# Two groups of expert gates behind every second late unit, four buffers of one-hots, and norm sums 128 columns wide

## The reference

```python
def rmsnorm(x, g):
    y = x * rsqrt(mean(x * x, axis=-1) + EPS)
    return y * g

def peer(h, w_query, sub_keys1, sub_keys2, expert_down, expert_up):
    # 8 heads, for each the best 16 of 128 x 128 experts by product keys
    ...
    gates = softmax(top_s)
    act = gelu(einsum("td,thkd->thk", h, expert_down[idx]))
    return einsum("thk,thkd->td", gates * act, expert_up[idx])
```

## Time and profile before

| | us |
|---|---|
| median of 3 runs (1384.83 to 1387.41) | 1386.22 |
| profiled execution, its own time | 1383.88 |
| its span in the trace | 1382.1 |
| TensorE busy | 1356.7 (98% of the span) |
| VectorE busy | 1032.1 (75%) |
| ScalarE busy | 863.1 (62%) |
| GpSimd busy | 652.3 (47%) |
| late stage, first to last `spread` | 804.6 to 1016.5 |

### The profile page before, as it was taken

The page is one execution under the profiler, slowest core; times in us unless marked ns, Lnnn a source line. Parts: engine busy times, 40 slices in busy tenths (PEclk is TensorE's granted clock), DMA queues, the critical chain, the costliest instruction groups (busy, mean ns, idle before and its releaser), DMA issues.

```text
span 1382.1 us, 30164 instructions
## 1 busy us (share of the span) xinstructions
PE 1356.7 (98%) x9200; PEld 1232.4 (89%) x9200; DVE 1032.1 (75%) x2272; ACT 863.1 (62%) x1825; POOL 652.3 (47%) x503
## 2 busy tenths in 40 slices
PE   7999999999999999999999999999999999999998
PEld 5799999999999988888888899999988888888886
DVE  7778868888888496548899678888876666666665
ACT  5668765555446666536666787777765555555554
POOL 4896793000005867698998887777720000000000
PEclk9999999999999999999999999999999999999998
DMA  9776565988883643565555554444456656666652
GB/s 340 279 253 225 203 241 183 332 323 320 334 331 119 215 138 107 183 229 182 183 196 184 182 169 153 154 160 157 152 167 196 189 193 196 191 191 195 194 188 89
DMA packets 79798, 283.83 MB, mean 205 GB/s; under 512 B 8821, under 2 KB 8949, under 8 KB 79610
## 3 DMA queue, kind: packets, MB, share of 16 engines
q1 hardware_dynamic: 79738, 283.07, 59.8%
HBM read 281.99 MB, written 1.05 MB: 205 GB/s over the span
## 4 chain that ended last, share of the span: by engine, by line
PE 66%; POOL 17%; issue 10%; DVE 4%; ACT 2%; DMA 1%; POOLq 0%; PEld 0%; PEldq 0%; SPq 0%; DVEq 0%
POOL w_lo L564 16%; PE psA L1868 15%; PE psA L1872 15%; PE psA L1871 15%; PE psD L1868 5%; PE psD L1871 5%; PE psD L1872 5%; PE psD L2363 1%; PE psD L2364 1%; PE psD L1918 1%; DVE arena L1549 1%; DMA xT<-x 1%; ACT w_hi L629 1%; DVE arena L1154 0%; PE psD L1921 0%
## 5 line engine op out<-in xcount | busy, mean ns | idle before, releaser
L629 ACT CAST w_hi<-raw 128x512 fp32r<-128x512 f32 x864 | 531.2, 620 | 430.6 <-PE psA L1868 251.3
L564 POOL TENSOR_TENSOR w_lo<-raw,w_hi 128x512 fp32r<-128x512 f32 x476 | 631.5, 1346 | 348.0 <-ACT w_hi L629 337.1
L1105 DVE TENSOR_TENSOR w_lo<-raw,w_hi 128x512 fp32r<-128x512 f32 x388 | 266.1, 691 | 152.6 <-ACT w_hi L629 151.3
L1868 PE MATMUL psA<-h_both,w_hi 128*128 128x256 f32 x960 | 279.5, 291 | 0.6 <-POOL w_lo L564 0.5
L1871 PE MATMUL psA<-h_both,w_hi 128*128 128x256 f32 x960 | 271.0, 282 | 0.0
L1872 PE MATMUL psA<-h_both,w_lo 128*128 128x256 f32 x960 | 270.9, 282 | 0.0
L1918 PE MATMUL psA<-h_both,w_hi 128*128 128x512 f32 x608 | 213.4, 396 | 0.4 <-POOL w_lo L564 0.4
L1868 PE MATMUL psA<-w_hi,u_hi 128*128 128x512 f32 x512 | 199.4, 389 | 0.4 <-DVE u_lo L1168 0.4
L1872 PE MATMUL psA<-w_hi,u_lo 128*128 128x512 f32 x512 | 199.2, 389 | 0.0
L1871 PE MATMUL psA<-w_lo,u_hi 128*128 128x512 f32 x512 | 199.2, 389 | 0.0
L1868 PEld LDWEIGHTS psA<-h_both,w_hi 128*128 128x128 f32 x960 | 183.4, 191 | 4.1 <-issue 1.5
(11 more groups left out here) (413 smaller groups left out, 2563.4 us busy)
## 6 DMA issues: line engine op xcount, KB each, us to landing
raw<-expert_down SPq DMA_DIRECT2D x128, 512.0 KB, 3.2
raw<-expert_up SPq DMA_DIRECT2D x128, 512.0 KB, 4.3
arena<-ada SPq DMA_DIRECT2D x96, 512.0 KB, 5.4
raw<-gateup SPq DMA_DIRECT2D x44, 512.0 KB, 5.4
raw<-feat SPq DMA_DIRECT2D x28, 512.0 KB, 3.7
raw<-win SPq DMA_DIRECT2D x24, 512.0 KB, 3.3
raw<-down SPq DMA_DIRECT2D x22, 512.0 KB, 6.0
raw<-wout SPq DMA_DIRECT2D x20, 512.0 KB, 3.3
```

Of the source, the lines that this page charges most:

```text
L564: nc.gpsimd.tensor_tensor(w_lo[:, s * HALF:(s + 1) * HALF], raw_half(n), w_hi[:, s * HALF:(s + 1) * HALF].bitcast(F32), ALU.subtract).then ...
L629: nc.scalar.copy(w_hi[:, n % SLOTS * HALF:(n % SLOTS + 1) * HALF], raw_half(n)).then_inc(hi_ready, 1)
L1105: V.tensor_tensor(w_lo[:, w], raw[:, n % 8 * HALF:(n % 8 + 1) * HALF], w_hi[:, w].bitcast(F32), ALU.subtract).then_inc(lo_ready, 1)
L1868: first = mm(o, w[0], m[0], start=start, stop=False, skip_group_check=True)
```

## The change

It makes four edits.

1. `GROUPS` goes from 2 to 4: four buffers of one-hots. Those of groups 0 to 3 are made ahead of the stage; VectorE's `group(g)` makes those of group g+4, and ScalarE lowers those of group k+4 behind the GELU of unit k (two groups each behind the last two units ahead of the stage).
2. TensorE makes no `spread` behind the first half of the even late units, and two behind that of the odd ones. The last two groups stay where they were.
3. The sums of `ssq_both` and of the final norm are 128 columns wide and not 2.
4. `keep_clock` with 2 matmuls ahead of `ssq_both`, and with 3 between the final sums and the final row spreads.

```diff
-        GROUPS = 2
-        hot = part(at_place("hot", M_AT, 2048, F16), 0, GROUPS, 2, GROUP, NK)
-        hot_lo = part(nc.alloc_sbuf_tensor_at("hot_lo", [P, 1024], F16, offset=late_at + 4 * 1024), 0,
+        GROUPS = 4
+        hot = part(at_place("hot", M_AT, 4096, F16), 0, GROUPS, 2, GROUP, NK)
+        hot_lo = part(nc.alloc_sbuf_tensor_at("hot_lo", [P, 2048], F16, offset=late_at + 4 * 1024), 0,
                       GROUPS, GROUP, NK)
...
                 if j >= P - LATE - 2:
-                    lower_hots((j - (P - LATE - 2)) * GROUP)
+                    for g in range(2):
+                        lower_hots(((j - (P - LATE - 2)) * 2 + g) * GROUP)
...
                 for j in range(4):
                     activate_late()
-                    lower_hots(i * (4 * GROUP) + (j + 2) * GROUP)
+                    lower_hots(i * (4 * GROUP) + (j + GROUPS) * GROUP)
...
             for j in range(3):
                 activate_late()
-                if j < 2:
-                    lower_hots(T - (2 - j) * GROUP)
...
-            one_hots(0)
-            one_hots(GROUP)
+            for g in range(GROUPS):
+                one_hots(g * GROUP)
...
                 gate_experts(g * GROUP)
-                one_hots(g * GROUP + 2 * GROUP)
+                one_hots(g * GROUP + GROUPS * GROUP)
                 multiply_late(late)
...
-            gate_experts(T - 2 * GROUP)
-            gate_experts(T - GROUP)
+            for g in range(N_GROUPS - GROUPS, N_GROUPS):
+                gate_experts(g * GROUP)
+                if g < N_GROUPS - 2:
+                    multiply_late(P - LATE + g)
...
                     for t in range(NT):
-                        last = mm(b[:, 2 * t:2 * t + 2], src[:, j, t * P:(t + 1) * P], weights[:, j, :],
+                        last = mm(b[:, t * P:(t + 1) * P].rearrange("p (n c) -> p n c", c=2),
+                                  src[:, j, t * P:(t + 1) * P],
+                                  weights[:, j, :].unsqueeze(1).broadcast_to([P, P // 2, 2]),
...
             first_banks = [Dr.bank(), Dr.bank()]
+            keep_clock(first_banks[0], 2)
             ssq_both(xn2, both_w, lambda: keep_clock(first_banks[0], 5))
...
-            for _ in range(LATE % LATE_TURN - 2):
-                unit(A, h_parts, beside=spread)
+            def spread_two(h):
+                if h == 0:
+                    spread(0)
+                    spread(0)
+            for k in range(LATE % LATE_TURN - 2):
+                unit(A, h_parts, beside=spread_two if k % 2 else None)
             with repeat(pe, LATE // LATE_TURN, {halves: 2 * LATE_TURN, A.count: LATE_TURN, groups: LATE_TURN}):
-                for _ in range(LATE_TURN):
-                    unit(A, h_parts, beside=spread)
+                for k in range(LATE_TURN):
+                    unit(A, h_parts, beside=spread_two if k % 2 else None)
...
-                    done = mm(psA[:, 0, 2 * t:2 * t + 2], U[:, j, t * P:(t + 1) * P], ones[:, 0:2],
+                    done = mm(psA[:, 0, t * P:(t + 1) * P], U[:, j, t * P:(t + 1) * P], ones[:, :],
...
             done.then_inc(sem("final_sums"), 1)
+            keep_clock(psA[:, BANKS - 1, :], 3)
             pe.wait_ge(sem("final_inverse"), 1)
```

More of the change, by code:

```diff
@@ L655, in roots_of @@
                     b = psA[:, A_AT[name] % BANKS, :]
-                    sums = b[:, 0:2 * NT].rearrange("p (t c) -> p c t", c=2)
+                    sums = b[:, 0:T].rearrange("p (t c) -> p c t", c=P)
                     nc.scalar.activation(roots[:, 0, :], sums[:, 0, :], ACT.Sqrt,
@@ L1064, in _ @@
             act.wait_ge(sem("final_sums"), 1)
-            nc.scalar.activation(roots[:, 0, :], psA[:, 0, 0:2 * NT].rearrange("p (t c) -> p c t", c=2)[:, 0, :],
+            nc.scalar.activation(roots[:, 0, :], psA[:, 0, 0:T].rearrange("p (t c) -> p c t", c=P)[:, 0, :],
                                  ACT.Sqrt, bias=eps[:, 0:1]).then_inc(sem("final_roots"), 1)
@@ L1785, in _ @@
             TURN = 12
-            at = N_GROUPS - 2 - (N_GROUPS - 2) // TURN * TURN
+            at = (N_GROUPS - GROUPS) % TURN
             for g in range(at):
                 group(g, P - LATE + g)
-            with repeat(dve, (N_GROUPS - 2 - at) // TURN, {hots: TURN, gates_n: TURN, late_n: TURN}) as i:
+            with repeat(dve, (N_GROUPS - GROUPS) // TURN, {hots: TURN, gates_n: TURN, late_n: TURN}) as i:
                 for g in range(TURN):
                     group(i * TURN + (g + at), i * TURN + (P - LATE + at + g))
-            gate_experts(T - 2 * GROUP)
-            gate_experts(T - GROUP)
+            for g in range(N_GROUPS - GROUPS, N_GROUPS):
+                gate_experts(g * GROUP)
+                if g < N_GROUPS - 2:
+                    multiply_late(P - LATE + g)
             lows.n = 2 * (UNITS - DVE_LOWERS)
```

## The result

The changed kernel takes 1400.85 us (median of 4 runs, 1399.8 to 1402.59), the kernel before 1386.82 (median of 4). The ratio is 1.0102, 95% interval 1.0085 to 1.0119: slower by 14.0 us, with some 12 to 16.5 allowed by the interval. The forecast was 1402.2, range 1395 to 1411.

A forecast was written before the change was run, and what follows sets the result against it. TensorE, busy 98% of the span, was taken as the bound. Late-stage waits +16.8, stage start +0.5, 0, and the end -1.3 gave +16.0 us on 1386.2: 1402.2 us, range 1395 to 1411.

The forecast's parts named there:

- The chain of helpers: Late stage: VectorE, ScalarE, GpSimd path delivers a lower half 0.53 us late; two units take 7.32 us against 6.76, +16.8 us.
- the link of 0.44 us: Late stage: ScalarE's next CAST starts 0.44 us behind VectorE's last one-hot; bounds 0.2 and 0.6.
- One remark beside the chain: Late stage, kernel before: the same path had 3.38 us and one group's 0.43 to spare.
- The start of the stage: Start of the late stage: two more sets of one-hots ahead of the first gates, +0.5 us, bounds 0 and 2.
- Fewer changes of format: Late stage, TensorE: pairs remove 31 of 64 fp16-to-fp32r returns at 0.08 us, 2.5 us less; bounds 0 and 3.1.
- The end: Final sums and row spreads: full clock with wide sums and clock-keeping matmuls, -1.3 us; otherwise rows delayed by 0.6.
- `ssq_both`: Norm sums ahead of the second block, wide with 2 added matmuls: sum 0, bounds -0.5 and +0.4 us.
- The sum: Whole kernel: 16.8 + 0.5 + 0 - 1.3 = +16.0 us, forecast median 1402.2 us.
- ScalarE does not hold the CASTs back: Late stage: path at most 4.85 us, not 5.38, so TensorE never waits; -3.8, 1382.4 us. Chance 0.08.
- A small wait: Late stage: path 4.9 to 5.0 us, waits of 0.1 us and saved returns cancel; within 3 us of 1386. Chance 0.04.
- The waits cost the clock: Late stage: TensorE's stops lower its granted clock; +11 us for a tenth of the pairs, +108 for all. Chance 0.04.
- The wide sums do not hold the clock: Norm stretches: the -1.3 becomes up to +0.6, 1404 us, within the forecast's range; no chance of its own given.

The follow-up runs named there:

- experiment 1: The changed kernel with ScalarE lowering group k+2, not k+4, behind the GELU of unit k: 1381.79 us, ratio to before 0.9975.
- experiment 9: The changed kernel with ScalarE lowering group k+3, not k+4, behind the GELU of unit k: 1381.51 us, ratio to before 0.9971.
- experiment 8: The changed kernel with one more 128x128 copy on ScalarE behind the lowering in every even turn: 1417.46 us, one run.
- experiment 3: The kernel before with edits 1 and 2 (the late stage) alone, sums narrow: 1404.69 us, ratio to before 1.0135.
- experiment 4: The kernel before with edit 2 alone: pairs on TensorE, two buffers of one-hots: 1407.57 us, ratio to before 1.0156.
- experiment 7: The kernel before with four buffers and one-hots and lowering four groups ahead, but one group behind each unit on TensorE: 1386.34 us, one run.
- experiment 2: The kernel before with edits 3 and 4 alone (wide sums, added clock-keeping), also called norms alone: 1383.67 us, ratio to before 0.9979.
- experiment 5: The kernel before with both sums 128 columns wide and no added clock-keeping matmuls: 1383.95 us, ratio to before 0.9988.
- experiment 10: The changed kernel with ScalarE lowering two groups ahead and without the 2 and 3 added clock-keeping matmuls: 1380.73 us, ratio to before 0.9967.

## Why the prediction was right, point by point

- **The chain of helpers.** It held link by link, none off by more than 0.02 us, and the period, 7.34 us against 7.32. 30 x (7.34 - 6.76) = 17.4 us where 16.8 was forecast. Experiments 1 and 9 take the link on ScalarE away and the loss goes; experiment 8 lengthens it and the loss grows one for one. That the link of 0.44 us, read at one spot, came out to the hundredth is partly luck: my own bounds for it were 0.2 and 0.6. One remark beside the chain is wrong by its own sum: before, TensorE was due at that half at L + 0.03 + 1.52 + 2 x 3.38 = L + 8.31, so the slack of the path was 2.9 us, and not 3.38 and 0.43. Nothing in the forecast was worked out from it.
- **The start of the stage.** 18.2 - 17.4 = 0.8 us against 0.5, within the bounds of 0 and 2.
- **Fewer changes of format.** Here a term was mis-sized. A pair without a wait takes 6.71 us and not 6.68: 0.05 us is saved where I had 0.08. Behind the last fp16 matmul of a group the next matmul starts 0.03 us later, where fp16 matmuls are 0.055 us apart; I counted the dear start of the second fp32r matmul and not this early start of the first. 31 x 0.05 = 1.6 us, and experiment 1's stage is 1.7 shorter than before.
- **The end.** -1.3 us forecast, -1.3 in the two traces (18.2 to 16.9). But with narrow sums and nothing added the end took 18.2 (before), 16.8, 18.8 and 17.2 us (experiments 3, 4 and 7), 17.75 on average: it is a gain in those executions in which the clock falls early enough, and I had read it from one trace as fixed. By these four traces the term is nearer to -0.8. That it came out at -1.3 in the pair of traces compared is luck.
- **`ssq_both`.** The step "sum 0, bounds -0.5 and +0.4" failed. From TensorE's first matmul of this stretch to the end of the row spread it is 6.36 us in the trace of before and 6.06 with wide sums and added matmuls, so -0.3, inside the bounds. But experiments 3, 4 and 7, with narrow sums too, took 8.37, 6.88 and 7.59: it depends on where the clock falls, and the term is -1.2 on average over the four narrow traces. Norms alone gave 2.9 us (1.7 to 4.2) and not 1.3; the two averages make 2.1 of it.
- **The sum.** The stage was 0.9 us dearer than its terms (18.2 against 17.3), the norms 1.6 cheaper (2.9 against 1.3); the errors partly cancel and leave +15.3. What remains to the +14.0 measured is within its interval of 12 to 16.5, as is the +16.0 of the forecast.
- **The rivals.** *ScalarE does not hold the CASTs back* would have needed a path 0.53 us shorter. Its time, 1382.4, is what experiment 1 measured (1381.8), where ScalarE indeed does not. *A small wait* would have been 0.1 us and not 0.54. *The waits cost the clock*: 31 waits in 230 us, and the granted clock 1.00 throughout. What the Trainium skill, TensorE: Matmul & The Clock Gate, "A second HAM failure mode: psum-queue depth-cycling", tells of another kernel, that short idle times between groups of matmuls make the clock go back and forth, did not show in this one: the trace has 0.38 us of them in every 7.34 and no fall. *The wide sums do not hold the clock*: they did, with 1.00 at 425 to 427 us and the last row spreads in 1.16 us.

## What to carry to other kernels

When a step is moved to a later turn, look on every engine at what is queued behind the instruction that waits for it, and count from the moved step to the first thing that the bounding engine needs from there; a buffer more does nothing while one engine's written order ties the two together. Compare that path with the time to when it is due: here it cost nothing up to that point (experiments 1, 7 and 9), and beyond it one for one in every turn (experiment 8). An engine's share of busy time says nothing of this: ScalarE was busy 62% of the span, and 0.44 us more at one place cost 0.44 us.

## What the runs showed that I had not expected

A float32 matmul with 2 moving columns takes as long as one with 128, 0.116 us a record, counts as busy, and yet the granted clock fell from 2.4 to 1.2 GHz during or behind a run of them, at different points in different executions: the same 32 records took 3.71 and 5.17 us. With 128 columns in the same matmuls it did not fall there in any of the seven traces. Only these two widths were run, so how many columns it takes is open.

The mean granted clock lay between 0.992 and 0.997 in all 59 runs of before, and between 0.999 and 1.000 in all but one (0.997) of the 48 runs of experiments 1, 2, 5, 9 and 10, which have wide sums. That made the kernel faster, but not clearly steadier. The 9 runs of experiment 1 lie only 1.8 us apart (1381.01 to 1382.82), where the 19 of before beside them lie 4.9 apart. But the 12 of experiment 5, at the same whole clock, lie 5.9 apart (1381.87 to 1387.78), as do the 23 of before beside them. Some of the scatter lies ahead of the late stage, where the transposes come at 796.3 to 800.9 us in the twelve traces; what causes it I did not find.
